# Sixteen experts on one core: the sample's down burst moves behind its gate and up bursts, and the turns are gathered behind it

## The reference, cut to what matters

```
gates, idx = lax.top_k(aff.T, cap)          # 128 rows (prompt), 32 rows (sample) per expert
xs  = t[idx]
hid = silu(xs @ w_gate[e]) * (xs @ w_up[e])
out = (hid @ w_down[e]) * gates
y[idx] += out
x = x + y
```

## Time and profile before

| | us |
|---|---|
| median of 3 runs | 2052.98 (2052.41 to 2054.71) |
| the profiled execution, its own time | 2055.39 |
| its span, first to last instruction | 2053.6 |
| one frame of the loop, product 0 to product 0 | 45.94 |

### The profile page before, as it was taken

One profiled execution on the slowest core, in us unless ns is written; L12 is line 12 of the kernel. 1 busy time (PEld: TensorE's weight loads), 2 busy tenths in 40 slices (PEclk: granted clock), 3 DMA queues, 4 the chain that ended last, 5 costly groups with the idle time before them and its releaser, 6 DMA issues.

```text
span 2053.6 us, 33280 instructions
## 1 busy us (share of the span) xinstructions
PE 2018.7 (98%) x13208; PEld 1671.2 (81%) x13208; DVE 1344.6 (65%) x1600; ACT 964.4 (47%) x1206; POOL 938.5 (46%) x664
## 2 busy tenths in 40 slices
PE   8999999999999999999999999899999999999997
PEld 8888888888889889888988888677777777777775
DVE  7865455456777477777755278677777677776674
ACT  7212211113555366666641133465665556656663
POOL 0985555566655377666642636413223222222221
PEclk9999999999999999999999999999999999999999
DMA  4223544333677622232135464778877788888873
GB/s 154 106 105 135 172 162 142 121 93 130 230 250 247 222 65 88 66 115 72 55 109 176 162 197 165 283 317 315 305 279 281 293 314 314 314 315 311 294 271 108
DMA packets 180585, 403.16 MB, mean 196 GB/s; under 512 B 16896, under 2 KB 99840, under 8 KB 180480
## 3 DMA queue, kind: packets, MB, share of 16 engines
q1 hardware_dynamic: 165744, 348.63, 46.3%
q0 software_dynamic: 7680, 20.98, 4.4%
q10 hardware_dynamic: 7056, 32.12, 4.4%
HBM read 322.38 MB, written 79.30 MB: 196 GB/s over the span
## 4 chain that ended last, share of the span: by engine, by line
PE 84%; DVE 6%; ACT 3%; DMA 2%; POOL 2%; issue 1%; SPq 0%; ACTq 0%; DVEq 0%; POOLq 0%
PE PS L1910 25%; PE PS L480 12%; PE PS L481 12%; PE PS L482 12%; PE PS L1941 8%; PE PS L1660 3%; PE PS L1643 1%; PE PS L1647 1%; PE PS L1644 1%; PE PS L1645 1%; PE PS L1646 1%; PE PS L1583 1%; PE PS L1466 1%; DMA w_raw<-in_w_out 1%; PE PS L2022 1%
## 5 line engine op out<-in xcount | busy, mean ns | idle before, releaser
L480 PE MATMUL PS<-act_hi,w_hi 128*128 128x256 f32 (+1 forms) x800 | 274.7, 343 | 1.5 <-issue 0.7
L481 PE MATMUL PS<-act_lo,w_hi 128*128 128x256 f32 (+1 forms) x800 | 269.7, 337 | 0.0
L482 PE MATMUL PS<-act_hi,w_lo 128*128 128x256 f32 (+1 forms) x800 | 269.2, 336 | 0.0
L1169 POOL TENSOR_SCALAR prob<-prob,small 128x1024 f32<-128x1024 f32 x64 | 185.6, 2900 | 111.6 <-DVE small L2896 111.6
L1269 POOL DMA_INDIRECT y_s<-ob_s,ixs_s x16 | 44.0, 2752 | 349.6 <-DVE ob_s L3189 349.6
L3092 DVE TENSOR_TENSOR elo<-raw,ehi 128x2048 fp32r<-128x2048 f32 x64 | 146.4, 2289 | 32.3 <-ACT ehi L2531 32.2
L1910 PE MATMUL PS<-ehi,xT_hi 128*128 128x512 f32 x520 | 164.2, 397 | 3.2 <-DVE elo L3092 2.3
L480 PEld LDWEIGHTS PS<-act_hi,w_hi 128*128 128x128 f32 x800 | 151.5, 189 | 18.2 <-issue 1.9
L482 PEld LDWEIGHTS PS<-act_hi,w_lo 128*128 128x128 f32 x800 | 151.2, 189 | 16.4
L481 PEld LDWEIGHTS PS<-act_lo,w_hi 128*128 128x128 f32 x800 | 151.6, 190 | 14.7 <-issue 0.7
L1910 PE MATMUL PS<-elo,xT_hi 128*128 128x512 f32 x520 | 160.6, 390 | 0.0
(11 more groups left out here) (415 smaller groups left out, 5491.4 us busy)
## 6 DMA issues: line engine op xcount, KB each, us to landing
raw<-in_w_gate SPq DMA_DIRECT2D x63, 1024.0 KB, 6.6
raw_more<-in_w_up SPq DMA_DIRECT2D x32, 1024.0 KB, 12.6
raw_w<-in_w_up SPq DMA_DIRECT2D x32, 1024.0 KB, 16.4
w_raw<-in_w_in SPq DMA_DIRECT2D x16, 1024.0 KB, 7.7
w_raw<-in_w_down SPq DMA_DIRECT2D x15, 1024.0 KB
stg<-in_w_down SPq DMA_DIRECT2D x15, 1024.0 KB, 7.9
gt<-in_w_down SPq DMA_DIRECT2D x15, 1024.0 KB, 9.9
raw_end<-in_w_down SPq DMA_DIRECT2D x15, 1024.0 KB, 14.4
```

The costliest lines, as they stand in the source:

```text
L480: pe.matmul(out, lh, rh, start=first, stop=False)
L481: pe.matmul(out, lh, rl, start=False, stop=False)
L482: return pe.matmul(out, ll, rh, start=False, stop=last)
L1169: pool.tensor_scalar(prob[:, n % 3], prob[:, n % 3], prec[:, c:c + 1], None, ALU.mult).then_inc(S["norm_pool"], 1)
```

## The change

The sample's down burst (expert e-1) moves from behind step 11 to straight behind the gate and up bursts, behind step 7, from frame 1 on. It writes bank 4 in place of bank 6, so TensorE waits there for `ob_act`, and it gets waits for the loads of its four slots. All turns, `turn_x`, `turn_h`, `turn_xs` and `turn_hs`, follow it there, in frame 15 too. Behind step 11 nothing is left but the next frame's step 0. On Vector `out` for the sample moves from step 1 of the frame behind to step 10 of the same frame, and `gated` is parted: the prompt's half stays in step 9, the sample's half goes to step 10. On Scalar, Silu of the prompt's gate goes from step 5 to step 8 and Silu of the sample's gate from step 8 to step 10. SyncE gets one more wait ahead of each down piece, since the burst is no longer the last reader of its slot. `out` and `hidden` on Scalar and `hidden` and `rows_few` on Vector stay where they are.

```diff
 # SyncE, load_piece
                     sp.wait_ge(S["e_few"], bursts(kind, e - 1) - 3 + kk)
+                    if kind == "d":
+                        sp.wait_ge(S["e_lo"], 12 * e + 1 + kk)
 # TensorE, few_product
-            def few_product(bs, few, slots, order=(0, 1, 2, 3)):
+            def few_product(bs, few, slots, order=(0, 1, 2, 3), loaded=None):
...
+                    if loaded is not None and n % 2 == 0:
+                        pe.wait_ge(S[f"e_in{slots[k // 2]}"], loaded)
 # TensorE, frame
-                    if l == 8 and not is1 and not is_last:
-                        pe.wait_ge(S["ob_act"], e - 1)
+                    if l == 8 and not is_last:
+                        pe.wait_ge(S["ob_dve"], e)
...
                     if l == 7 and not is_last:
                         pe.wait_ge(S["xs_dve"], e + 1)
-                        if not (is0 or is1):
-                            pe.wait_ge(S["ob_dve"], e - 1)
                         few_product(6, lambda k: quarters(xT_s, k), ...)
                         few_product(7, lambda k: quarters(xT_s, k), range(4, 8))
-                        if more and not is0:
-                            pe.wait_ge(S["silu_p"], e + 1)
-                            turn_x(e + 1)
-                    if l == 11 and not is_last:
-                        pe.wait_ge(S["silu_s"], e + 1)
-                        few_product(6, lambda k: quarters(hT_s, k), range(8, 12))
-                        if more:
+                        if not is0:
+                            if not is1:
+                                pe.wait_ge(S["ob_act"], e - 1)
+                            few_product(4, lambda k: quarters(hT_s, k), range(8, 12), loaded=16 * e)
+                            if more:
+                                pe.wait_ge(S["silu_p"], e + 1)
+                                turn_x(e + 1)
                             turn_h(e)
                             pe.wait_ge(S["mul_s"], e + 1)
-                            turn_xs(e + 1)
+                            if more:
+                                turn_xs(e + 1)
                             turn_hs(e)
...
-                    if isinstance(e, int) and e == E - 1 and l == 10:
-                        turn_h(E - 1)
-                        turn_hs(E - 1)
 # Scalar, frame
-                    if l == (6 if is0 else 5):
-                        act.wait_ge(S["e_main"], 4 if is0 else q - 1)
+                    if l == (6 if is0 else 8) and not is_last:
+                        act.wait_ge(S["e_main"], 4 if is0 else 12 * e)
...
-                    if l == (7 if is0 else 8) and not is_last:
+                    if l == (7 if is0 else 10) and not is_last:
                         act.wait_ge(S["e_few"], bursts("g", e))
 # Vector, frame
-                    if l == (8 if is_last else 1) and not (is0 or is1):
-                        out(e - 2, 6)
...
                     if l == 9 and not is_last:
-                        gated(e)
+                        gated_p(e)
+                    if l == 10 and not is_last:
+                        gated_s(e)
+                        out(e - 1, 4)
```

More of the change, by code:

```diff
@@ L3141, in frame @@
                     if is1 and l == 0:
-                        gated(0)
+                        gated_p(0)
+                        gated_s(0)
                     if is1 and l == 1:
                         rows_few(1)
-                    if l == (8 if is_last else 1) and not (is0 or is1):
-                        out(e - 2, 6)
                     if l == 2 and not is0:
@@ L3158, in frame, with gated_p, gated_s @@
                     out(e - 1, 7)
-            def gated(e):
+            def gated_p(e):
                 dve.wait_ge(S["e_main"], 8 if isinstance(e, int) and e == 0 else 12 * e + 4)
+                dve.wait_ge(S["silu_p"], e + 1)
+                dve.tensor_tensor(hid[:], bank(2, D), hid[:], ALU.mult).then_inc(S["mul_p"], 1)
+            def gated_s(e):
                 dve.wait_ge(S["e_few"], bursts("u", e))
-                dve.wait_ge(S["silu_p"], e + 1)
                 dve.wait_ge(S["silu_s"], e + 1)
-                dve.tensor_tensor(hid[:], bank(2, D), hid[:], ALU.mult).then_inc(S["mul_p"], 1)
                 dve.tensor_tensor(hid_s[:], bank(7, GN), hid_s[:], ALU.mult).then_inc(S["mul_s"], 1)
```

## The result

The changed kernel takes 2075.43 us (median of 4 runs, 2074.61 to 2077.03) against 2053.60 for the kernel before (4 runs): 21.8 us slower, ratio 1.0106, 95% interval 1.0094 to 1.0118. The forecast was 2075.7, on a time before of 2052.98 (three of the four runs), with a range of 2066 to 2083. The profiled execution's own time is 2075.18, its span 2073.4.

The account below looks back on a forecast made before the run. TensorE alone was taken to set the time. Gain of 3.9 us in 15 frames, loss of 23.5 at 14 borders and 3.1 in frame 16 gave +22.7 on 2052.98: 2075.7 us, range 2066 to 2083.

Parts of the forecast that it names:

- The saving on TensorE: Twelve products in a row with fewer switches: a frame of 45.52 us without waits, 0.42 less than 45.94.
- The four waits for loads: New waits between the down burst's groups of 16 matmuls: 0.04 us each, 0.16 a frame, bounds 0 and 0.32.
- The landing of 16.4: Time a down piece's load was taken to need at most, in us, against 30 us until its burst.
- The border: Counting from T, product 11's end: products 2 and 3 wait for `elo`; 1.68 us lost per frame, 14 times, 23.5 us.
- Frame 16: `out(14)` in the first step, no longer covered by the down burst, makes the second product late: 3.1 us.
- The sum: Loop gain, borders and frame 16 together: -3.9 + 23.5 + 3.1 = +22.7 us, bounds +18.2 and +25.1.
- A: Rival: the merge pays and the border doesn't stall; about 2048 us; chance 0.03.
- B: Rival: only product 2 is late, 0.40 us a frame, so gain and delay about cancel; 2055 to 2058; chance 0.04.
- D: Rival: burst waits for a load, or step 8 for `ob_s`; 1 us a frame, about 2090; chance 0.10.
- E: Rival: `out` starts sooner or Vector's small operations pack tighter, 0.3 to 0.6 us a frame less; about 2069; chance 0.12.
- C: Rival: TensorE's clock drops in the 14 new border gaps of 1.1 us; another 38 us, about 2114; chance 0.03.

Follow-up runs that it names:

- e4: Changed kernel with Scalar's `out` in step 3 (frame 16: behind the third `ehi`) and Vector's copies hT_s and xT_s in step 10: 2047.68 us, ratio to before 0.9965.
- e8: Kernel before with one part of the change alone, Silu of the prompt's gate in step 8 instead of step 5: 2053.45 us, ratio 0.9997.
- e7: Changed kernel with `turn_h`, `turn_xs` and `turn_hs` back behind step 11 in frames 1 to 14, down burst in its new place: 2058.46 us, ratio to before 1.0018.
- e1: Changed kernel with Scalar's `out` in step 3, behind the `ehi` of steps 2 and 3, in frames 2 to 15: 2057.99 us, ratio to before 1.0017.
- e3: Changed kernel with Vector's copies hT_s and xT_s moved to step 10 of the frame ahead: 2065.01 us, 10.4 less than the changed kernel.
- e5: Changed kernel with one more Vector copy of 128x256 ahead of xT_s in step 2 of frames 2 to 15: 2079.32 us.
- e6: Changed kernel with one more Scalar copy of 128x1024 ahead of hT_hi in step 2 of frames 2 to 15: 2074.28 us.
- e2: Changed kernel with Scalar's `out(14)` two steps later, behind the third step's `ehi`, in frame 16 alone: 2071.57 us.

## Why the prediction was right, by its own steps

- **The saving on TensorE** was given as 0.42 us a frame without waits. e4, where no product waits at the border, shows 45.94 - 45.51 = 0.43; 0.10 of it is Silu's (e8).
- **The four waits for loads** were put at 0.04 each between bounds of 0 and 0.08. They cost 0, the lower bound. This term was mis-sized by 0.16 a frame, 2.4 us in all; the 0.08 by which one row of turns was longer than another was hardly the price of the two waits behind it, since in e7 `turn_h` with the same waits behind it takes 1431.25 - 1430.38 = 0.87, and `turn_x` took 0.85. The landing of 16.4 was the median of up pieces and no upper bound: the down pieces of the changed kernel landed in 16.9 to 20.8 us (medians of its page). Against the 30 us to their burst this changed nothing.
- **The border** was worked out as product 2 at T + 5.70, product 3 at T + 9.70, 1.68 us a frame lost. The trace has T + 5.67, T + 9.67 and 1.66. That the chain runs through `out`, the `ehi` of step 2 and Vector's own row of work is shown by taking away its links (e1, e3, e4, e7) and by lengthening it on Vector (e5) and beside it on Scalar (e6).
- **Frame 16** was given 3.1 us for a late product. From the first product's start the delay was 2.6, since `out` started at T + 0.2 there (2043.62, with the product before over at 2042.97 + 0.45 = 2043.42) and the first product itself 0.16 late. Another 1.7 came on top from the clock. The prediction had weighed the clock for the gaps of 1.1 us and had put its cost at nothing for this gap of its own, nearly three times as long.
- **The sum.** In the loop 47.17 - 45.94 = 1.23 a frame instead of 1.42, for 14 borders 17.2 us; the tail from the gate burst of frame 15 is 38.08 us against 2039.14 - 2004.98 = 34.16, 3.9 more. That makes 21.1, and the medians differ by 21.8. The profiled executions differ by 19.8, since this one was 1.45 ahead at the gate burst of frame 0, which the change does not explain, and still 1.3 at that of frame 1. The forecast of 22.7 was thus 14 x 0.19 = 2.7 too high in the loop and 1.1 too low from frame 15's bursts on (3.1 - 0.26 = 2.8 against 3.9). The 1.6 too much that this leaves is nearly cancelled by the 0.7 between the frames and the medians and by the base of 2052.98 where four runs give 2053.60: that the forecast met the median within 0.3 us is luck, that it met the size of the loss is not. Of the kernel before, the gate burst of frame 15 and the last burst:

```profile
2004.98 3.66 PE L1941 MATMUL PS<-raw,xT_s 128*32 128x256 f32 x64
...
2039.14 3.66 PE L1941 MATMUL PS<-raw,xT_s 128*32 128x256 f32 x64
```

- **The rivals.** A (no stall) and B (only product 2 late) are out by the timeline. D (a load or `ob_s` not in time) is out: no idle time ends with either. E (a tighter row of work) is out by the start times. C, the clock, came true in one place of fifteen, and not in one that it named: the 14 gaps of about 1 us left the clock at 1.00 (in every stretch from 1360 to 2040), the one gap of 2.4 us did not. The price in that place was 1.7 us, not a whole product's 2.7.

## What to carry to other kernels

A break on the engine that is the bound (a burst of small matmuls, a row of transposes) is slack for all the others, and they may have work written into just that place. Before such a break is moved or merged away, write down for the border, in start-to-start times, what each other engine does in its written order from the event that releases it to the instruction that the bound engine wants next; the gain here was 0.43 us a frame and the uncovered chain cost 1.66. Then move that work along: what has long been ready (here two copies, ready half a frame earlier) to where its engine idles, and what is not urgent (here `out`) behind what is. With both done the same change gains 0.35% where it had lost 1.06%. Of the 0.43 us, 0.10 belong to the later Silu (e8) and need no merge.

## What the runs showed of the hardware

- The same gap of 2.4 us ahead of the same product in frame 16 stands in the profiles of the changed kernel, e1, e3, e5, e6 and e7. In five of the six the product behind it ran in part at 1.2 GHz (pairs of matmuls 0.85 us apart, 4.4 to 4.5 us for 12 matmuls), in e5 it ran at 2.4 GHz throughout (0.46, 2.86 us). Where the gap was taken away (e2, e4) the slow product was gone too. Gaps of 0.97 to 1.31 us at the frames' borders of the changed kernel, e2, e5 and e6 did not show it. So behind a gap of 2.4 us the clock may fall or not from one execution to the next; what decides it was not tried. The Trainium skill, TensorE: Matmul & The Clock Gate, section on HAM oscillation, warns of idle gaps that let the clock fall; frame 16 shows such a fall, behind a gap shorter than those the section warns of, and here the measurement decides. The fall and rise of the clock that its section on a second failure mode tells of, from brief and frequent idle times between groups of matmuls, is not seen with the 14 short gaps here, one in 47 us; more frequent ones were not run.
- A semaphore wait whose count is reached, written between groups of small matmuls (54 ns apart), is not seen in TensorE's start times: 0.86 us for 16 matmuls with it and 0.87 without.
